# The output projection of a hybrid decoder layer with tokens on partitions, and an earlier load of two input panels

## The reference, cut to what matters

```python
h = _rms_norm(x, p['ln_mix_pre'])
qa, ka, va, qkvb, bb, ab, zb, qc, gates = jnp.split(h @ p['w_in'], _split_points(), axis=-1)
...
up = jnp.einsum('blnc,ncd->blnd', branches, p['w_branch'])
gate = jax.nn.sigmoid(gates.reshape(Bsz, L, N_BRANCH, D_MODEL))
mix = jnp.sum(gate * up, axis=2) @ p['w_out']
x = x + _rms_norm(mix, p['ln_mix_post'])
h = _rms_norm(x, p['ln_ffn_pre'])
gt, uf = jnp.split(h @ p['w_ffn_in'], 2, axis=-1)
f = (jax.nn.silu(gt) * uf) @ p['w_ffn_out']
x = x + _rms_norm(f, p['ln_ffn_post'])
```

## Time and profile before

| | us |
|---|---|
| median of 3 runs (lowest, highest) | 2189.09 (2187.46, 2193.29) |
| the profiled execution | 2202.99 |
| its span | 2201.2 |
| PE busy | 2106.1 (96% of the span) |
| PEld, DVE, ACT, POOL busy | 2056.9, 984.8, 527.0, 770.8 |
| chain that ended last | PE 85%, DVE 7%, ACT 4%, DMA 2% |

### The profile page before, as it was taken

The page is one execution under the profiler, slowest core; times in us unless marked ns, Lnnn a source line. Parts: engine busy times, 40 slices in busy tenths (PEclk is TensorE's granted clock), DMA queues, the critical chain, the costliest instruction groups (busy, mean ns, idle before and its releaser), DMA issues.

```text
span 2201.2 us, 34799 instructions
## 1 busy us (share of the span) xinstructions
PE 2106.1 (96%) x13727; PEld 2056.9 (93%) x13727; DVE 984.8 (45%) x1666; ACT 527.0 (24%) x1161; POOL 770.8 (35%) x326
## 2 busy tenths in 40 slices
PE   6899999999999999999999997699999999999998
PEld 6899999999999999999899997699999999999997
DVE  5655540355555555311347902734353443534435
ACT  4233621233333333221032213400000000000002
POOL 2334874211111111121143434343434344344444
PEclk8999999999999999999799998799999999999999
DMA  4223332433122232253274323211111111111114
GB/s 156 88 77 98 117 107 98 132 98 98 58 75 82 81 98 64 70 170 100 88 256 161 107 81 110 101 49 48 48 38 48 48 48 42 44 48 39 55 39 158
DMA packets 227416, 193.82 MB, mean 88 GB/s; under 512 B 24715, under 2 KB 200459, under 8 KB 227298
## 3 DMA queue, kind: packets, MB, share of 16 engines
q1 hardware_dynamic: 213186, 182.72, 26.7%
q10 hardware_dynamic: 14128, 9.65, 1.4%
HBM read 146.26 MB, written 47.09 MB: 88 GB/s over the span
## 4 chain that ended last, share of the span: by engine, by line
PE 85%; DVE 7%; ACT 4%; DMA 2%; issue 1%; POOL 1%; SPq 0%; ACTq 0%; DVEq 0%; POOLq 0%
PE psum L1402 23%; PE psum L918 13%; PE psum L1469 11%; PE psum L1016 7%; PE psum L1088 6%; PE psum L1168 4%; PE psum L1412 4%; PE psum L1394 4%; PE psum L1137 2%; ACT pr L1739 1%; PE psum L1126 1%; DMA brw<-s_br 1%; PE psum L971 1%; PE psum L940 1%; PE psum L1110 1%
## 5 line engine op out<-in xcount | busy, mean ns | idle before, releaser
L807 POOL TENSOR_TENSOR wsp<-raw,kc 128x1024 fp32r<-128x1024 f32 x137 | 329.7, 2407 | 1362.3 <-PE psum L1088 433.9
L1402 PE MATMUL psum<-actD,wsp 128*128 128x352 f32 x3168 | 517.7, 324 | 0.9 <-DVE actD L2435 0.9
L1402 PEld LDWEIGHTS psum<-actD,wsp 128*128 128x128 f32 x3168 | 511.5, 189 | 1.0 <-DVE actD L2435 1.0
L810 POOL TENSOR_TENSOR wsp<-raw,wsp 128x1024 fp32r<-128x1024 f32 x137 | 343.5, 2508 | 10.7
L918 PE MATMUL psum<-actT,wsp 128*128 128x352 f32 (+1 forms) x1800 | 295.7, 325 | 6.5 <-POOL wsp L810 6.5
L918 PEld LDWEIGHTS psum<-actT,wsp 128*128 128x128 f32 (+1 forms) x1800 | 285.7, 186 | 12.2 <-POOL wsp L810 6.8
L2484 DVE TENSOR_TENSOR accT<-accT,psum 128x352 f32<-128x352 f32 x504 | 241.7, 520 | 50.1 <-PE psum L1469 50.1
L1469 PE MATMUL psum<-fT,wsp 128*128 128x352 f32 x1512 | 249.8, 323 | 0.4 <-DVE accT L2484 0.4
L1469 PEld LDWEIGHTS psum<-fT,wsp 128*128 128x128 f32 x1512 | 244.0, 188 | 0.7 <-DVE accT L2484 0.7
L1088 PE MATMUL psum<-actT,wsp 128*128 128x352 f32 x1152 | 216.4, 333 | 0.0
L2467 DVE TENSOR_TENSOR fr<-psum,sg 128x352 f32<-128x352 f32 x66 | 34.6, 524 | 378.7 <-PE psum L1402 375.9
(11 more groups left out here) (406 smaller groups left out, 2403.5 us busy)
## 6 DMA issues: line engine op xcount, KB each, us to landing
raw<-in_w_in SPq DMA_DIRECT2D x100, 256.0 KB, 3.9
raw<-in_w_ffn_in SPq DMA_DIRECT2D x88, 256.0 KB, 3.1
gat<-s_gate SPq DMA_DIRECT2D x12, 1056.0 KB, 5.1
raw<-in_w_ffn_out SPq DMA_DIRECT2D x44, 256.0 KB, 2.7
s_gate<-gst SPq DMA_DIRECT2D x48, 176.0 KB, 1.8
s_qkv<-y SPq DMA_DIRECT2D x12, 528.0 KB, 3.0
brw<-s_br SPq DMA_DIRECT2D x3, 2112.0 KB, 9.9
raw<-in_w_branch SPq DMA_DIRECT2D x24, 256.0 KB, 5.6
```

The costliest lines, as they stand in the source:

```text
L807: pool.tensor_tensor(wsp[:, slot, 0], raw[:, slot], ones.unsqueeze(1).to_broadcast([P, KT, P]), ALU.mult).then_inc(w_hi, 1)
L810: pool.tensor_tensor(wsp[:, slot, 1], raw[:, slot], wsp[:, slot, 0].bitcast(F32), ALU.subtract).then_inc(w_lo, 1)
L1402: mm = pe.matmul(psum[:, bank, 0:CH], wsp[:, slot, a, k, :], actD[:, h, k, CH * c:CH * c + CH], start=(k == 0 and q == 0), stop=(k == KT - ...
```

## The change

The output projection swaps its operands: a tile of 128 tokens of the mixed activations is the stationary operand and a row block of `w_out` (128 x 1024) is the moving one, 512 columns at a time. A tile is 8 blocks x 3 passes x 2 halves = 48 matmuls, nine tiles are 432, and the result has tokens on partitions, so `turn_rows` and the copies of L1877 are gone, and `norms` reads PSUM. All eight row blocks of `w_out` are split ahead and stay resident in `wo_mk`, `wo_br`, `wo_ac`, `wo_top` and one `wsp` slot, in memory that other tiles free at different times. POOL takes them between the branch panels in the order W_SEQ. Before the first tile PE waits for all three chunks of the last branch half (`g_ev`, 3 + UO). The last tile's add goes from POOL to DVE. The memory of ln_ffn_post's gain is gone from `gn`; it is loaded late into `gp`. In the opening, the loads of panels 2 and 3 stand right behind the load of the memory rows, panel 2 is split into `wm`, the chunks of the first two panels get banks 0, 1, 2, 7, 0, 1, and the 12 small transposes of the convolution state move behind the fifth chunk.

```diff
+    W_SEQ = [("b", j) for j in range(5)] + [("o", 0), ("b", 5), ("o", 1), ("b", 6), ("o", 2), ("b", 7), ("b", 8), ("b", 9), ("o", 3),
+             ("b", 10), ("o", 4), ("b", 11), ("o", 5), ("o", 6), ("o", 7)]
...
+    FIRST_BANK = (0, 1, 2, 7, 0, 1)
...
         sp.dma_start(xin[:, 0:2, :], mem_view.rearrange("t p d -> p t d")).then_inc(x_in[0], 16)
+        load_b(2)
+        load_b(3)
...
         sp.wait_ge(p_in, 96)
-        for n in range(2, 4):
-            load_b(n)
...
+        def load_wo(k):
+            n = W_N["o", k]
+            sp.wait_ge(w_lo, n + 1)
+            for h in range(2):
+                sp.dma_start(raw[:, n % 2, 4 * h:4 * h + 4, :], io["w_out"][P * k:P * k + P, 512 * h:512 * h + 512].rearrange("p (k n) -> p k n", n=P)).then_inc(w_in[n % 2], 16)
...
         for j in range(12):
             if j + 2 < 12:
-                load_wb(j + 2)
+                load_seq(W_N["b", j + 1] - NPD + 1, W_N["b", j + 2] - NPD + 1)
                 load_q(j + 2)
...
-        for m in range(8):
-            n = NPO + m
-            load_w(n, [(raw[:, n % 2, 4 * h:4 * h + 4, :], wov[:, 4 * h:4 * h + 4, P * m:P * m + P]) for h in range(2)])
+        load_seq(W_N["b", 11] - NPD + 1, 20)
...
+        sp.wait_ge(b_lo, 1 + MIX_N(2, 7) + 1)
         for t in range(4):
             x_io(t)
...
         sp.wait_ge(g_mm, 6 + UF + 6 * NF)
         sp.wait_ge(t_xst[0], 16 * 6)
         sp.wait_ge(t_xst[1], 16 * 5)
+        sp.dma_start(gp[:], io["ln_ffn_post"].partition_broadcast(P)).then_inc(b_in, 16)
         sp.dma_start(xf[:, 0:NT], s_x1[0:NT].rearrange("t p d -> p t d")).then_inc(r_in[0], 16)
...
-        split_at(2, 0, 64, 6 + 5)
+        pool.wait_ge(w_in[0], 64)
+        pool.tensor_tensor(wm[:, 0], raw[:, 0], ones.unsqueeze(1).to_broadcast([P, KT, P]), ALU.mult).then_inc(w_hi, 1)
+        pool.wait_ge(w_hi, 3)
+        pool.tensor_tensor(wm[:, 1], raw[:, 0], wm[:, 0].bitcast(F32), ALU.subtract).then_inc(w_lo, 1)
...
+        for kind, j in W_SEQ:
+            if kind == "b":
+                slot = (NPD + j) % 2
+                pool.wait_ge(g_mm, 6 + UD + (6 * (j - 1) if j > 0 else -3))
+                split_to(W_N[kind, j], *(wsp[:, slot, a].rearrange("p k n -> p (k n)") for a in range(2)))
+            else:
+                if j == 0:
+                    pool.wait_ge(f_st, F_ST)
+                if j == 3:
+                    pool.wait_ge(b_lo, 1 + BR_N(3, 0))
+                if j in (5, 6):
+                    pool.wait_ge(b_lo, 1 + MIX_N(0, (1, 3)[j - 5]) + 1)
+                if j == 7:
+                    pool.wait_ge(g_mm, 6 + UO)
+                split_to(W_N[kind, j], *(wo_part(j, a) for a in range(2)))
+        split_at(NPF, NPF % 2, 32 * (NPF // 2) + 32, 6 + UO - 6)
+        for t in range(NT):
+            add_row(pool, t, t % 2, P)
+        pool.wait_ge(t_tr, NT + 1)
+        split_at(NPF + 1, (NPF + 1) % 2, 32 * ((NPF + 1) // 2) + 32, 6 + UO)
...
+        def out_rows(t, slot, rows):
+            pe.wait_ge(t_y, t + 1)
+            c = (P * t + rows - 1) // CH
+            for k in range(KT):
+                if t == 0:
+                    pe.wait_ge(w_lo, W_N["o", k] + 3)
+                if t in (0, 2, 5):
+                    pe.wait_ge(b_lo, 1 + MIX_N(c, k) + 1)
                 for q, (a, h) in enumerate(passes):
+                    for half in range(2):
+                        mm = pe.matmul(psum[0:rows, 2 * slot + half, :], actD[:, h, (k + 4) % 8, P * t:P * t + rows],
+                                       wo_part(k, a)[:, 512 * half:512 * half + 512],
+                                       start=(k == 0 and q == 0), stop=(k == KT - 1 and q == 2))
             mm.then_inc(t_tr, 1)
+
+        pe.wait_ge(g_ev, 3 + UO)
...
+        for t in range(NT + 1):
+            out_rows(t, t % 2, P if t < NT else NS)
             if t >= 2:
+                turn_back(t - 2, t % 2, P)
+        pe.wait_ge(w_lo, NPF + 3)
+        for c in range(2):
+            pe.wait_ge(u_lo, 2 + 3 * c + 3)
+            full_chunk(NPF % 2, c, 6 + c)
+        turn_back(NT - 1, 1, P)
+        turn_back(NT, 0, NS)
...
         norms(NT - 1, 1, first=NS)
+        dve.wait_ge(t_x1, NT)
+        add_row(dve, NT, 0, NS)
         norms(NT, 0, first=0, second=NS)
```

More of the change, by code:

```diff
@@ L363, in build @@
     UO = UD + 72
-    UF = UO + 24
+    UF = UO
+    W_SEQ = [("b", j) for j in range(5)] + [("o", 0), ("b", 5), ("o", 1), ("b", 6), ("o", 2), ("b", 7), ("b", 8), ("b", 9), ("o", 3),
+             ("b", 10), ("o", 4), ("b", 11), ("o", 5), ("o", 6), ("o", 7)]
+    W_N = {item: NPD + i for i, item in enumerate(W_SEQ)}
     ORDER = (0, 1, 2)
@@ L631, in load_wb, with load_seq @@
                     sp.dma_start(dst[:, 2 * h:2 * h + 2], src.rearrange("(k p) n -> p k n", p=P)[:, 2 * h:2 * h + 2]).then_inc(w_in[n % 2], 16)
+        def load_wo(k):
[3 more added lines that the diff above has]
+                sp.dma_start(raw[:, n % 2, 4 * h:4 * h + 4, :], io["w_out"][P * k:P * k + P, 512 * h:512 * h + 512].rearrange("p (k n) -> p k n", n=P)).then_inc(w_in[n % 2], 16)
+        def load_seq(first, last):
+            for kind, j in W_SEQ[first:last]:
+                (load_wb if kind == "b" else load_wo)(j)
         def load_br(r):
@@ L933, in first_chunk @@
         def first_chunk(n, c, read):
+            bank = FIRST_BANK[2 * c + n]
             pe.wait_ge(w_lo, n + 3)
@@ L1871, in _ @@
                 act.activation(actD[:, 0, m - 4, cols], accT[:, m, cols], ACT.Copy).then_inc(b_hi, 1)
-        for m in range(8):
-            if m == 0:
-                act.wait_ge(b_lo, 1 + MIX_N(2, 7) + 1)
-            for c in range(3):
-                act.wait_ge(g_mm, 6 + UO + 3 * m + c + 1)
-                act.activation(accT[:, m, CH * c:CH * c + CH], psum[:, c, 0:CH], ACT.Copy).then_inc(g_ev, 1)
         def rows_psum(slot, rows):
@@ L1883, in norm1 @@
             act.wait_ge(t_tr, t + 1)
-            act.activation(jk[0:rows, slot, :], rows_psum(slot, rows), ACT.Square, accum_out=ns[0:rows, slot, 0, 0:1]).then_inc(t_sq, 1)
+            act.activation(jk[0:rows, :], rows_psum(slot, rows), ACT.Square, accum_out=ns[0:rows, slot, 0, 0:1]).then_inc(t_sq, 1)
         def root1(t, slot, rows):
@@ L1891, in norm2 @@
             act.wait_ge(t_x1, t + 1)
-            act.activation(jk[0:rows, slot, :], xr[0:rows, t % 4, :], ACT.Square, accum_out=ns[0:rows, slot, 1, 0:1]).then_inc(u_sq, 1)
+            act.activation(jk[0:rows, :], xr[0:rows, t % 4, :], ACT.Square, accum_out=ns[0:rows, slot, 1, 0:1]).then_inc(u_sq, 1)
         def root2(t, slot, rows):
@@ L1950, in _ @@
             act.wait_ge(t_tr, 9 + t + 1)
-            act.activation(jk[0:rows, t % 2, :], rows_psum(slot, rows), ACT.Square,
+            act.activation(jk[0:rows, :], rows_psum(slot, rows), ACT.Square,
                            accum_out=ns[0:rows, slot % 2, slot // 2, 0:1]).then_inc(t_sq, 1)
```

129 lines of the change are left out of this document (62 added, 67 removed).

## The result

The changed kernel takes 2157.9 us (median of 4 runs, 2153.42 to 2168.56); the kernel before, run beside it, 2191.19 (4 runs, 2187.46 to 2202.86). The ratio is **0.9842 [0.9815, 0.9868]**, 33.3 us less between the medians. The profiled execution took 2157.78 us (span 2156.0), 45.2 less than the one of before.

What follows compares the result with a forecast made beforehand. PE, busy 96% of the span, was taken as the bound. Opening -10.5, branch products +8, start wait through norms -31.2 and clock +2 sum to -31.7, taking 2189.1 to 2157 us; range 2143 to 2173.

Steps and rivals of the forecast that it cites:

- the w_out part: Everything from the branch products on, without the opening's gain: -21.2 us.
- Opening: Start up to panel 2: PE's waits for panel 2's split and for ACT go, -10.5 us (-7 to -13).
- Branch products: Matmuls ahead of the w_out product: POOL's added splits hold up DVE, and PE with it, +8 us (+3 to +13).
- the price of a split: Branch products: each split, two POOL instructions, costs DVE about 2 x 1.7 = 3.4 us.
- the +16: Branch products: the cost if the port's loser is blocked for whole instructions, a split costing DVE 5 us; +16 instead of +8.
- The wait at the start: Start of the w_out product: PE waits until DVE reads the last branch chunk, +8 us (+5 to +12).
- The product: The w_out product: 432 matmuls of 512 columns at 0.2295 us, 99.1 us for 92.6; six turn_back between tiles add 6.2.
- The rival with latency as pitch: The w_out product does not pipeline: matmuls come every 0.392 us, in all +38, 2227 us; chance 0.05.
- The norms' tail: Behind the last tile's product: the chain of the last norms up to the FFN's chunk 2 takes 15.7 us.
- The clock: The w_out product: after 8 us of idleness a piece may run at 1.2 GHz, +2 us (0 to +5).
- What costs nothing: After the product: loading gp ahead of xf, DVE's wait for stores and POOL's later FFN split stay hidden, 0 us.
- the rival in which the port costs more: POOL and DVE hold each other up: branch +13 to +16, start +12, clock +5; 2171 to 2175 us; chance 0.17.

Runs made afterwards that it cites:

- opening_only: The kernel before with only the opening's part of the change (early loads, panel 2 into wm, new banks): 2185.68 us, ratio 0.9968.
- early_loads_only: The kernel before with the early loads and panel 2 split into wm, but the old banks and old place of the small transposes: 2188.84 us, ratio 0.9978.
- projection_only: The changed kernel with the opening of the kernel before: 2174.14 us, ratio 0.9899 to before.
- tile0_banks: The changed kernel with tile 0 of the w_out product in banks 6 and 7, waiting for all chunks only before tile 1: 2150.01 us, ratio 0.9797.
- port_doubled: The changed kernel with POOL running the first instruction of the splits of o1 to o4 two more times each: 2164.19 us, ratio 0.9853.
- old_form: The changed kernel with the branch stage's splits in before's form (8 x 128 blocks, 128 columns of ones): 2167.48 us, ratio 0.9859.
- changed_yardstick: The changed kernel, unaltered, run again on the same chip and in the rounds of old_form_again: 2164.73 us, ratio 0.9869.
- old_form_again: The kernel of old_form run again, beside changed_yardstick on one chip: 2169.69 us, ratio 0.9889.
- banks_and_tail: The changed kernel with tile 0 in banks 6 and 7 and chunk 0 of the FFN's second panel ahead of the last turn_back: 2146.53 us, ratio 0.9758.
- changed_again: The changed kernel, unaltered, run once more on the same chip as the first follow-up kernels: 2163.9 us, ratio 0.9861.

## Why the prediction was right, and where it was not

The median came out at 2157.9 us for 2157.0 forecast, inside the range of 2143 to 2173, and the split into parts held: -9.5 for the opening by the runs (-11.4 in the profile) for -10.5, and -21.0 for the w_out part for -21.2. Some of that is terms whose errors cancel, and the hit to 0.9 us is luck: the difference was -33.3 us for -31.7, from a kernel before that measured 2.1 us more than the one that the forecast started from. In two later groups of runs the difference was -31.3 and -31.1.

- **Opening, right in the sum, in part by luck.** All three waits went, as opening_only shows. Panel 2 at 59.91 is in the forecast's 59 to 62, though it came before 59 in eight of the ten other profiles with this opening. The 11.4 us of the profile are 8.4 us less idle time, since 2.9 us of waits for turned tiles came up that the sum did not have, and 3.0 us less for the same work at a granted clock of 0.92 instead of 0.82, which the sum had as a bound only. In time it is -9.5 or -7.0. The 1.64 us by which POOL might hold up the norms fit the 2.9 us of waits for turned tiles after against 1.3 in opening_only, but as both have POOL's instructions there, that cause is not shown.
- **Branch products, the step that failed.** The forecast was +8 us, with "more waits for L2401", and it named an unchanged branch part as a sign of being wrong. PE's waits in the stage are 9.1, 9.5 and 8.8 us in three profiles of the changed kernel, against 8.8 before, 8.5 in early_loads_only and 10.6 in opening_only: no change. The stage's length is 153.8 to 154.7 us there against 149.8 to 153.3 with the old code, so between nothing and +5, and none of it in the sum of the waits. In projection_only and tile0_banks, with the same branch code, it is 156.4 and 156.9 us with 10.2 and 10.7 of waits. In port_doubled and old_form both the length and the waits are clearly larger.

  What failed is the price of a split. The prediction took a hold of 1.7 us for each POOL instruction from the earlier trace rows, beside one of 2.47 us, where the diff writes it in another form that takes 1.89. Five splits more at 3.4 us were to cost DVE 17 us; DVE's work in the stage rose from 108.1 us to 111.3 (113.0 in changed_yardstick). With the form of the price (old_form) it is 118.4 and 120.0 us, PE's waits become 12.8 and 13.2 us, the stage 157.7 to 159.8, and the time rises by 5.0 on the same chip: the form that the prediction priced costs nearly what it said. The form is not all of the miss. An estimate by the prediction's own sum, with 0.5 us less for each split, still leaves DVE some 5.5 us behind instead of 10.5, and nothing of that shows in the sum of the waits; what takes it up was not tried.

  The number per panel and the shared port were right, since L2450 rose from 974 to 1118 ns. That is 48 x 0.144 = 6.9 us of DVE time. The Trainium skill ("SBUF — State Buffer", Who interferes with whom) says that the loser of the port is blocked for the whole instruction. The trace agrees for an instruction (7.82 us for four `lo_mix` while POOL ran back to back), but the +16 made from it counted a full block for each of POOL's, and DVE's work rose by far less.
- **What the branch part did cost, which the sum did not have.** The 3.6 us of the table are 0.3 us of waits and the rest PE's clock. In the kernel after the longest wait for L2448 is 2.87 us, before it was 1.69; the clock was then at half for 3.3 us, and the 72 matmuls behind the wait took 13.37 us where a panel takes 11.80. Every profile with the new branch code has this except port_doubled's, none with the old code has it:

```profile
1173.60:1176.90 3.30, 3.30 (x14) 3.30 (x13) 3.23 (x4) 0.00 (x0) 2.13 (x1) 0.51 0.00 0
```

That is 1.6 us. The length of the wait alone does not decide it, since in port_doubled the clock stayed at 1.00 behind a wait of 3.35 us. About as much again stands behind the wait of 3.97 us for L2445 (2.25 before), but opening_only with the old branch code has that too (4.16 us), so the splits did not bring it.
- **The wait at the start, right in kind and 2.9 us short.** 10.92 us for 8, within 5 to 12. The bound of +12, "four POOL instructions in a row, each of which lets one DVE instruction through", is what happened with three of them, from 0.3 us before PE's end. tile0_banks confirms the cause and its one condition: only the banks were late.
- **The product, right.** The product with its `turn_back` took 107.7 us. The forecast was 99.1 + 6.2 = 105.3, and the clock adds 2.0 in tile 0. A matmul of 512 columns had a median of 392 to 397 ns as forecast, and a tile at full clock took 11.15 us for 48 matmuls, 0.232 us each for 0.2295. The rival with latency as pitch (0.392) is dead. The gap formula of the Trainium skill ("TensorE: Matmul & The Clock Gate", Back-to-back issue gap), 216 ns, which the section gives for an isolated matmul, is not borne out: they came every 232 ns at a granted clock of 1.00. PE waited for nothing between tiles.
- **The norms' tail, right.** 14.6 us to chunk 2 for 15.7.
- **The clock, a little short.** +2 forecast; 2.0 in tile 0, and 2.2 more from chunk 2 on, where the clock is at half again for 6.8 us, most of them in the FFN's first matmuls (before, this place was at 1.00). What the clock took in the branch products stands above:

```profile
1371.30:1378.10 6.80, 5.72 (x24) 5.61 (x25) 3.46 (x3) 2.48 (x4) 0.00 (x0) 0.51 0.59 163
```

- **What costs nothing, right.** `xf` was issued at 2107.90, 0.4 us behind `gp`, and landed 14.4 us later, and the first add came at 2128.14, waiting for DVE's norm and not for a transfer:

```profile
2128.14 2.36 POOL L462 TENSOR_TENSOR xf<-xf,yr 128x1024 f32<-128x1024 f32 x1 [15.59 <-DVE yr L2561]
```

The profile's sum: -11.4 + 3.6 - 27.0 + 2.2 = -32.6 for a forecast of -31.7. The forecast has 4.4 too much cost in the branch part, 1.1 too much in the tail and 0.9 too little gain in the opening, against 2.9 too little cost at the start, 2.2 of clock and 0.4 in the product.

Two sums of the prediction do not come out. The terms of the rival in which the port costs more add up to 12 to 15 us (2169 to 2172) and not to 14 to 17. The bounds of its own terms, all low or all high, give 2138 to 2175, so the 2143 to 2171 is a narrower choice and not their sum.

## What to carry to other kernels

A wait that gathers several releases of buffers is set by the last instruction in the other engine's order, here 10.9 us behind; give the first piece of the next stage buffers that nobody holds and put the wait behind it (-13.9 us). Price a moved instruction by a row in its new form, not by that of the operation it replaces: 1.89 or 2.40 us for the same product made 4 us of waits and 5 us of time. Look at the clock behind a wait too: here one wait became 1.2 us longer and the matmuls behind it 1.6 us slower, with the sum of the waits unchanged. Before a stage is read as faster or slower, compare its granted clock in several executions, since the same code moved by 12 us between two profiles.

## What was not expected of the hardware

- POOL's multiplication of 128x1024 elements by ones takes 1.89 us as one row of 1024 with one column of ones repeated, and 2.40 us as 8 rows of 128 with 128 columns of ones. The subtraction behind it takes 2.45 to 2.49 us in the mean of 116 in either shape. Whether the number of rows or the ones' pattern makes it was not tried apart.
- PE's clock was granted at half from 4.8 us after it fell idle until 4.0 us after it had started again; without the idle stretch it stayed at 1.00.
- A piece of some 23 us at half clock in the middle of the program, ahead of the branch products, stood in the profiles of before, old_form_again and banks_and_tail and not in those of the kernel after or opening_only; changed_again, the same kernel as the one after, had 14 us at 0.51 a little later. What brings it is open.
